# Retrieval on Trainium2: one of six one-hot passes per tile moved from VectorE to GpSimd, on a buffer of its own

## What is computed

```
s = einsum('nhpd,pkd->nhpk', q, sub_keys)              # two halves p of 128 keys
v_top, i_top = lax.top_k(s, 16)                        # 16 values and key numbers per half
cand = v_top[:, :, 0, :, None] + v_top[:, :, 1, None, :]    # 256 candidates
cidx = i_top[:, :, 0, :, None] * 128 + i_top[:, :, 1, None, :]
f_v, f_p = lax.top_k(cand, 16)                         # 16 of them
e = take_along_axis(cidx, f_p)                         # 16 experts of 16384
g = softmax(f_v)
out = sum over 128 experts of g * gelu(u_tab[e] . x) * v_tab[e]
```

## Time and profile before

| | us |
|---|---|
| median of 3 runs | 2819.33 |
| lowest, highest | 2811.58, 2819.66 |
| the profiled execution, its time | 2813.79 |
| its span | 2812.1 |
| DVE busy / POOL busy / PE busy in the span | 1763.2 / 859.0 / 1873.1 |

### The profile page before, as it was taken

How to read it: one execution, slowest core, us unless ns; L and a number is a source line. 1 busy time by engine, 2 the same in 40 slices (tenths; PEclk the granted TensorE clock), 3 DMA queues, 4 the chain that set the end, 5 groups by cost and what they waited for, 6 DMA issues and landing times. The chain is left out here.

```text
span 2812.1 us, 27454 instructions
## 1 busy us (share of the span) xinstructions
PE 1873.1 (67%) x7795; PEld 1065.9 (38%) x7795; DVE 1763.2 (63%) x3931; ACT 674.5 (24%) x2035; POOL 859.0 (31%) x827
## 2 busy tenths in 40 slices
PE   7999799699837659943776055656865247258474
PEld 3466466444412213311332044446622136246411
DVE  3444464711178955666799756647896888779813
ACT  2010366300123223312332112212221122223200
POOL 1000142200034522222535322214424775544301
PEclk9999899899868979976979577775597555555586
DMA  5131310054158978788889889887896999999763
GB/s 148 25 101 62 130 54 2 1 192 152 53 243 354 388 305 323 294 343 315 354 328 411 335 308 362 313 298 298 343 358 234 356 414 361 363 382 419 290 219 120
DMA packets 200930, 727.84 MB, mean 259 GB/s; under 512 B 39786, under 2 KB 83331, under 8 KB 133899
## 3 DMA queue, kind: packets, MB, share of 16 engines
q0 software_dynamic: 84096, 572.96, 51.1%
q1 hardware_dynamic: 115514, 148.89, 15.5%
q10 hardware_dynamic: 1168, 4.23, 0.4%
HBM read 717.42 MB, written 12.66 MB: 260 GB/s over the span
## 5 line engine op out<-in xcount | busy, mean ns | idle before, releaser
L3285 ACT ACTIVATE ex_coef<-ex_dots 128x1 f32<-128x1 f32 x512 | 103.5, 202 | 1056.8 <-DVE ex_dots L3257 1041.4
L3225 POOL DMA_INDIRECT ex_pairs<-in_uv_tab,e_idx x147 | 190.4, 1295 | 544.6 <-POOLq L3122 246.6
L3225 POOL DMA_INDIRECT branch_rows_t<-in_uv_tab,e_idx x171 | 209.9, 1227 | 280.6 <-DVE heads_t L3252 172.9
L3225 POOL DMA_INDIRECT heads_t<-in_uv_tab,e_idx x146 | 182.1, 1247 | 267.1 <-DVE heads_t L3252 161.7
L1336 PE MATMUL cs_pp<-cs_ch,xn_t 128*128 128x256 f32 x512 | 137.4, 435 | 175.8 <-DMA cs_ch<-in_cache_cmp_kv 175.8
L3257 DVE CUSTOM_DVE_ANT_0 branch_rows_t<-branch_rows_t,heads_t 128x1024 f32<-128x1024 f32 x171 | 208.5, 1220 | 52.0 <-DMA branch_rows_t<-in_uv_tab,e_idx 49.3
L819 PE MATMUL in_acc<-in_w,xn_t 128*128 128x512 f32 (+7 forms) x560 | 207.7, 526 | 5.9 <-POOLq L177 4.4
L3257 DVE CUSTOM_DVE_ANT_0 ex_pairs<-ex_pairs,heads_t 128x1024 f32<-128x1024 f32 x147 | 179.6, 1222 | 43.5 <-DMA ex_pairs<-in_uv_tab,e_idx 40.9
L3257 DVE CUSTOM_DVE_ANT_0 heads_t<-heads_t 128x1024 f32<-128x1024 f32 x146 | 178.0, 1220 | 45.9 <-DMA heads_t<-in_uv_tab,e_idx 43.6
L1336 PEld LDWEIGHTS cs_pp<-cs_ch,xn_t 128*128 128x128 f32 x512 | 112.5, 223 | 205.2 <-DMA cs_ch<-in_cache_cmp_kv 110.8
L3252 DVE SCALAR_TENSOR_TENSOR heads_t<-branch_rows_t,ex_coef,heads_t 128x1024 f32<-128x1024 f32 x126 | 161.4, 1281 | 10.8 <-DMA is_w<-tmp_w 5.5
(11 more groups left out here) (722 smaller groups left out, 3538.1 us busy)
## 6 DMA issues: line engine op xcount, KB each, us to landing
cs_ch<-in_cache_cmp_kv SPq DMA_DIRECT2D x256, 128.0 KB
fq_mg_wg<-in_w_gate SPq DMA_DIRECT2D x6, 2048.0 KB, 17.5
in_w<-in_w_in SPq DMA_DIRECT2D x4, 2048.0 KB, 11.3
first_w<-in_w_gate SPq DMA_DIRECT2D x3, 2048.0 KB, 8.1
fp_wb<-in_w_branch SPq DMA_DIRECT2D x6, 1024.0 KB, 10.2
fp_wg<-in_w_gate SPq DMA_DIRECT2D x3, 2048.0 KB, 8.0
fq_mg_wb<-in_w_branch SPq DMA_DIRECT2D x6, 1024.0 KB, 19.7
fs_mg_wb<-in_w_branch SPq DMA_DIRECT2D x6, 1024.0 KB, 9.9
```

Of the source, the lines that this page charges most:

```text
L3225: pool.indirect_dma_start(out=pair(s), out_offset=None, in_=i["uv_tab"], in_offset=bass.IndirectOffsetOnAxis(ap=idx[:, t, m:m + 1], axis=0 ...
L3285: act.activation(c, dots[:, t, m:m + 1], ACT.Gelu_apprx_tanh).then_inc(gelu_done, 1)
```

## The change

`hot`, the buffer of the one-hot rows, is doubled, one half for each digit. VectorE makes the one-hot rows of the second digit first (in the same piece as `fa` and `faf`, and without waiting for itself behind it) and tells GpSimd by `split_done`. GpSimd multiplies them by the second half's key numbers, in place, and tells VectorE by `hot_done`. VectorE does the three passes of the first digit meanwhile, waits for `hot_done`, and sums the second digit. GpSimd gets a program in each of the four retrieval stages; in the stages that lie beside the mixing it is due at fraction 0.92, or at 132/140 of a tile.

```diff
-        hot = self.sb(f"{tag}_pk_hot", [P, HP, PTOP, PTOP], F32, ctx)
+        hot = self.sb(f"{tag}_pk_hot", [P, 2, HP, PTOP, PTOP], F32, ctx)
...
             c.link(dve.tensor_copy(faf[:r, :, h], fa[:r, :, h]))
+            dve.tensor_tensor(hot[:r, 1, h], faf[:r, 1, h].unsqueeze(3).to_broadcast(full),
+                              iota_f[:r].unsqueeze(1).unsqueeze(1).to_broadcast(full), ALU.is_equal).then_inc(split_done, 1)
             yield
-            for a in range(2):
-                c.link(dve.tensor_tensor(hot[:r, h], ..., ALU.is_equal))
-                yield
-                c.link(dve.tensor_tensor(hot[:r, h], hot[:r, h], i2[:, :, a, :]..., ALU.mult))
-                yield
-                c.link(dve.tensor_reduce(sel[:r, a, h], hot[:r, h], AX, ALU.add))
-                yield
+            c.link(dve.tensor_tensor(hot[:r, 0, h], ..., ALU.is_equal))
+            yield
+            c.link(dve.tensor_tensor(hot[:r, 0, h], hot[:r, 0, h], i2[:, :, 0, :]..., ALU.mult))
+            yield
+            c.link(dve.tensor_reduce(sel[:r, 0, h], hot[:r, 0, h], AX, ALU.add))
+            yield
+            dve.wait_ge(hot_done, turn_of(n, heads) + 1)
+            c.link(dve.tensor_reduce(sel[:r, 1, h], hot[:r, 1, h], AX, ALU.add))
+            yield
...
+        def match(pool, n, heads=(0, HP)):
+
+            r, h, k, m = rows[n], slice(*heads), turn_of(n, heads), heads[1] - heads[0]
+            full = [r, m, PTOP, PTOP]
+            second = ixf[:r, 2 * heads[0]:2 * heads[1]].rearrange("p (h s) k -> p h s k", s=2)[:, :, 1, :]
+            pool.wait_ge(split_done, k + 1)
+            pool.tensor_tensor(hot[:r, 1, h], hot[:r, 1, h], second.unsqueeze(2).to_broadcast(full), ALU.mult).then_inc(hot_done, 1)
...
+            @block.gpsimd                       # retrieve_first
+            def _(pool):
+                part["match"](pool, 0, heads)
...
+            @block.gpsimd                       # retrieve_second_half
+            def _(pool):
+                yield 0.92
+                part["match"](pool, 0, heads)
...
+            @block.gpsimd                       # retrieve_rest
+            def _(pool):
+                for n in range(n_rest):
+                    yield (n + 132 / STEPS) / n_rest
+                    part["match"](pool, tile + n)
```

More of the change, by code:

```diff
@@ L2999, in retrieval @@
         s_ps = self.ps(f"{tag}_pk_s_ps", [P, 4, 4, NKEY], ctx)
-        mm, out_done, taken, tile_done, chain, diff_done, exp_done = (self.sem(f"{tag}_{n}") for n in (
-            "mm", "out", "taken", "tile", "chain", "diff", "exp"))
+        mm, out_done, taken, tile_done, chain, diff_done, exp_done, split_done, hot_done = (self.sem(f"{tag}_{n}") for n in (
+            "mm", "out", "taken", "tile", "chain", "diff", "exp", "split", "hot"))
         c = Chain(None, chain)
@@ L3083, in pick @@
             c.link(dve.tensor_copy(faf[:r, :, h], fa[:r, :, h]))
+            dve.tensor_tensor(hot[:r, 1, h], faf[:r, 1, h].unsqueeze(3).to_broadcast(full),
+                              iota_f[:r].unsqueeze(1).unsqueeze(1).to_broadcast(full), ALU.is_equal).then_inc(split_done, 1)
             yield
-            for a in range(2):
-                c.link(dve.tensor_tensor(hot[:r, h], faf[:r, a, h].unsqueeze(3).to_broadcast(full),
-                                         iota_f[:r].unsqueeze(1).unsqueeze(1).to_broadcast(full), ALU.is_equal))
-                yield
-                c.link(dve.tensor_tensor(hot[:r, h], hot[:r, h], i2[:, :, a, :].unsqueeze(2).to_broadcast(full), ALU.mult))
-                yield
-                c.link(dve.tensor_reduce(sel[:r, a, h], hot[:r, h], AX, ALU.add))
-                yield
+            c.link(dve.tensor_tensor(hot[:r, 0, h], faf[:r, 0, h].unsqueeze(3).to_broadcast(full),
+                                     iota_f[:r].unsqueeze(1).unsqueeze(1).to_broadcast(full), ALU.is_equal))
+            yield
+            c.link(dve.tensor_tensor(hot[:r, 0, h], hot[:r, 0, h], i2[:, :, 0, :].unsqueeze(2).to_broadcast(full), ALU.mult))
+            yield
[4 more added lines that the diff above has]
+            yield
             flat = lambda x: x[:r, h].rearrange("p h k -> p (h k)")
@@ L3112, in gate @@
             dve.wait_ge(tile_done, done)
-        return {"tag": tag, "rows": rows, "scores": scores, "keep": keep, "soft": soft, "pick": pick, "gate": gate, "idx_done": idx_done,
+        return {"tag": tag, "rows": rows, "scores": scores, "keep": keep, "soft": soft, "pick": pick, "match": match, "gate": gate, "idx_done": idx_done,
                 "chain": c, "keys_t": keys_t, "halves": halves}
```

## The result

| | median us | lowest to highest | against before |
|---|---|---|---|
| before | 2819.33 | 2811.58 to 2819.79 | |
| after | 2835.51 | 2825.80 to 2838.48 | 1.0057, interval 1.0034 to 1.0080 |

The rows are five executions of each kernel. The kernel became slower by 16 us, 0.57%. The forecast was +12.3 us, 0.44%, which lies in both intervals.

A forecast was written before the change was run, and what follows sets the result against it. It took DMA and VectorE, both nearly full during retrieval, as the bound. Terms +1.0 (heads 0 to 3), +3.6 (step 22), +6.0 (tiles 1 to 3) and +1.7 (step 147) gave +12.3 us: 2831.6 us, range 2811 to 2839.

The forecast's parts named there:

- Part 1: VectorE's picks: one multiply less each, 1.23 us for four heads, 2.29 for eight, 9.3 us in all.
- Part 2: Length of GpSimd's multiply: 4.3 us for 2048 columns, 2.2 for 1024, the geometric middle of far-apart bounds.
- the lower bound: GpSimd's multiply at its copies' rate, 1.9 us for 2048 columns and 1.0 for 1024; sum about +3.5 us.
- Part 3: In each pick, GpSimd's reading pass blocks VectorE's two-input pass: +1.0 us for four heads, +2.0 for eight.
- The side-by-side rivals: No blocking in the picks: with the queue's cost -4.1 us, chance 0.22; without it -9.3 us, chance 0.10.
- Part 4: GpSimd's queue: new waits hold back gathers, +3.6 us at step 22 (pick's 1.0 included), +1.7 at step 147.
- the wait at step 22: GpSimd, taking up tile 1's stage, must wait for the end of `gate`, so gathers 22 to 25 go out late.
- Steps 19 to 44: Second half of tile 0, its pick and late gathers: forecast +3.6 us, between worked-out ends +2.9 and +4.4.
- the long step of 4.0 us: Between dots 29 and 30 before; if it does not recur, the loss there is +2.9 instead of +4.4 us.
- Step 147: Start of tiles 2 and 3: GpSimd waits for the preceding stage's last copy, delaying gathers 147 to 150; +1.7 us.
- Steps 60, 178, 210: GpSimd's multiplies in tiles 1, 2, 3: later gathers stay covered and cost nothing, unless the pass exceeds 7 us.
- Carried to the end: Retrieval stages: a delay or gain at a stage's end moves all that follows, to the end of the span.

The follow-up runs named there:

- write_only: Kernel after, but GpSimd fills the second digit's rows with zeros instead of multiplying, reading nothing (other rows are gathered); ratio 1.0002.
- reorder: `late_free`, with VectorE doing the first digit's one-hot and multiply before the releasing one-hot pass, so only its sum runs beside GpSimd; ratio 1.0018.
- cut_by_head: `late_free`, with GpSimd's multiply cut into one instruction for each head, eight for a full tile; ratio 1.0059.
- late_free: Kernel after, without GpSimd's wait for earlier stages beside the mixing, and its half-tile multiply ahead of gather 24 instead of 21; ratio 1.0005.
- one_input: Kernel after, but GpSimd multiplies the second digit's rows by 1.0, one input instead of two (expert numbers wrong); 2835.41 us in one execution.
- free_only: Kernel after, without GpSimd's wait for earlier stages beside the mixing, its half-tile multiply still ahead of gather 21; 2827.26 us in one execution.
- buffer_only: Kernel before with the doubled buffer alone, all six passes on VectorE; ratio 1.0014.
- after_again: Kernel after, unchanged, run once more beside before; ratio 1.0033, median 2825.30 us.

## Why the prediction was right

- **Part 1**, 9.3 us of multiplies less on VectorE: the five instructions went, but VectorE's busy time grew by 7.4 us, since the blocked passes are longer by 16.6. The saving exists where nothing blocks: in `write_only` a full tile gains 2.5 to 2.7 us.
- **Part 2**, GpSimd's pass, taken as the middle between 1.9 and 9.6 us: 4.3 and 2.2 forecast, 4.50 and 2.34 measured unblocked. The 4497 ns of the Trainium skill (GPSIMD Engine Reference, 3.1 Elementwise) agree with 4.50. As what a VectorE pass loses it measured 4.18 us (5.40 - 1.22) and 2.03 us (3.25 - 1.22), as by these figures GpSimd's pass begins some 0.2 us ahead of the blocked record, and VectorE goes on some 0.1 us before GpSimd's ends. That the middle of two ends a factor of five apart came within some 6% is luck. The sum at the lower bound is also a slip: with the second pick at 1.0 us too it is -0.2 - 1.2 + 2.4 + 1.7 = +2.7, not +3.5.
- **Part 3**, the blocking and who goes first: shown. Removing GpSimd's reads (`write_only`), giving it a one-input neighbour (`reorder`) and cutting it into pieces (`cut_by_head`) removed it, the last down to one piece. The last two stand on `late_free`, in which the dots still last 5.40 us, so its other edits are not what removed it. The Trainium skill (SBUF — State Buffer, Who interferes with whom) puts the same: two-input VectorE against reading GpSimd, one instruction at a time; this case's runs agree, but for the earlier release in `one_input`. The side-by-side rivals fall. The term was over-sized: +1.5 to +1.7 for a full tile against 2.0, +0.6 for the first pick against 1.0, since the released pass is issued without a wait of its own behind it and the block is 4.18, not 4.3. `write_only` gives the first of these: a full tile gains 2.5 there, not 2.29, and 4.18 - 2.5 = 1.7.
- **Part 4**, the queue: the mechanism is right and the wait at step 22 is the larger part (`free_only`). Steps 19 to 44 cost +4.8 and +4.4 against 3.6, at or over the upper end worked out (+4.4): the long step of 4.0 us, which I half counted on to vanish, moved and did not vanish (in `after` it is the step from dot 27 to 28 instead of 29 to 30; dot 29 stands at +10.6, dot 44 at +9.1, from +4.3 at dot 19). Step 147: +1.9 and +1.4 against 1.7. Steps 60, 178, 210 cost nothing, as forecast: dots 60 and 61 are shifted as dot 59 is. In `cut_by_head`, where GpSimd is taken for over 7 us, dot 61 did wait, as part 4 says.
- **Carried to the end**: not quite. Between steps 178 and 206 1.1 us were given back, in the kernels with a queued multiply and in those without; I had not foreseen it (`buffer_only` -0.5, `late_free` -1.9). In `after_again` 6.5 us more were given back between dots 62 and 146. Nor do the whole times follow the places: `write_only` and `reorder` show no gain that their intervals could tell.
- **Open**: +10.8 and +9.4 us behind dot 215, where nothing is changed. The buffer's size is excluded as a large cause; whether it is the spread of single executions or something of the change was not settled. The agreement of the 16 us with the 12.3 is so far in part luck: the forecast is right for the places of the change, which sum to 12.1 and 11.2 us, and it put the other stretches at 0, which moved by as much. The second comparison gives 0.33%, some 9 us.

## What to carry to other kernels

Before a pass goes from VectorE to GpSimd, ask what VectorE does beside it: if that reads two SBUF operands, and GpSimd's pass reads SBUF at all, they run one after the other, and VectorE stands for nearly all of GpSimd's pass (4.18 of 4.50 us here). Beside a sum, which has one input, nothing was blocked; but VectorE then waited 2.49 us for GpSimd, so the move gained nothing. Passes other than the sum were not tried beside it. And where GpSimd issues the gathers, every wait in front of its new piece, those of the scaffolding too, is a wait of the gathers: look at which it already passes for free. GpSimd's pass must also be short enough for the gathers behind it: 6.47 us was, 10.51 us was not.

## What was not expected of the hardware

- GpSimd's single-scalar pass of one input is slower than its multiply of two: 5.2 us or more behind L3087 against 4.2 to 4.5 us for 2048 columns, and it blocked VectorE 3.3 us of this (`one_input`).
- A memset of 2048 columns on GpSimd (1.81 us) ran inside a two-input VectorE pass with neither longer (`write_only`).
- Pieces of 256 columns last 0.72 us each where nothing blocks them and start 0.68 us apart (`cut_by_head`); eight of them would so take some 5.5 us, an estimate, against 4.50 in one (`reorder`).
